# A two-layer diffusion backbone on one core: the start, the order of the input chunks, the queueing of small VectorE work, and the last chunk pairs of layer 1 in halves of 128 tokens

## What is computed

```python
for l in range(DEPTH):
    sh1, sc1, gt1, sh2, sc2, gt2 = adaln(c, w_ada[l], b_ada[l])
    hx = modulate(rms_norm(x, g_mix[l]), sh1, sc1)
    hc = modulate(rms_norm(ctx, g_mix[l]), csh1, csc1)
    px = split_cols(hx @ w_in[l], IN_SIZES)
    ...
    x = x + gt1 * mixer_output(px, y_attn, ...)
    x = x + gt2 * conv_ffn(modulate(rms_norm(x, g_ffn[l]), sh2, sc2), w_up[l], ...)
return rms_norm(x, g_final)
```

## Time and profile before

| | us |
|---|---|
| median of three runs | 1308.53 (1308.24 to 1309.39) |
| profiled execution | 1308.54 |
| its span in the trace | 1306.8 |
| PE busy | 1260.5 |
| DVE busy | 884.4 |
| ACT busy | 550.9 |
| POOL busy | 291.7 |
| granted TensorE clock, mean | 0.991 |

### The profile page before, as it was taken

The page is one execution under the profiler, slowest core; times in us unless marked ns, Lnnn a source line. Parts: engine busy times, 40 slices in busy tenths (PEclk is TensorE's granted clock), DMA queues, the critical chain, the costliest instruction groups (busy, mean ns, idle before and its releaser), DMA issues.

```text
span 1306.8 us, 20012 instructions
## 1 busy us (share of the span) xinstructions
PE 1260.5 (96%) x7718; PEld 1092.8 (84%) x7718; DVE 884.4 (68%) x1205; ACT 550.9 (42%) x872; POOL 291.7 (22%) x247
## 2 busy tenths in 40 slices
PE   4999999999999999999999999989989998999997
PEld 3788777777788798888888888989878998999997
DVE  4698678753699777662889664475676666665654
ACT  4322255553423245331223342344566645643543
POOL 0003699210233001111001110003871230220220
PEclk8999999999999999999999999999999998999999
DMA  9466311222366425662646663245333543664560
GB/s 376 155 224 201 121 61 61 73 65 76 108 201 242 124 71 183 190 216 76 205 161 195 195 216 134 66 125 174 114 105 100 194 160 130 200 217 139 183 209 33
DMA packets 50339, 198.76 MB, mean 152 GB/s; under 512 B 5584, under 2 KB 6992, under 8 KB 49104
## 3 DMA queue, kind: packets, MB, share of 16 engines
q1 hardware_dynamic: 50256, 197.62, 45.9%
HBM read 196.55 MB, written 1.05 MB: 151 GB/s over the span
## 4 chain that ended last, share of the span: by engine, by line
PE 84%; DVE 9%; ACT 4%; issue 2%; DMA 0%; SPq 0%; DVEq 0%; ACTq 0%
PE psA L522 24%; PE psA L524 24%; PE psA L523 24%; DVE w_lo L1268 2%; ACT w_hi L958 2%; PE psB L522 2%; PE psB L524 2%; PE psB L523 2%; DVE acc L1549 2%; DVE small L1562 1%; PE psA L773 1%; PE psB L801 1%; PE psB L789 1%; PE psB L704 1%; PE psB L543 1%
## 5 line engine op out<-in xcount | busy, mean ns | idle before, releaser
L522 PE MATMUL psA<-h_hi,w_hi 128*128 128x256 f32 (+1 forms) x1544 | 523.7, 339 | 10.1 <-DVE w_lo L1268 4.0
L524 PE MATMUL psA<-h_hi,w_lo 128*128 128x256 f32 (+1 forms) x1544 | 516.8, 335 | 0.0
L523 PE MATMUL psA<-h_lo,w_hi 128*128 128x256 f32 (+1 forms) x1544 | 516.7, 335 | 0.0
L1268 DVE TENSOR_TENSOR w_lo<-raw,w_hi 128x1024 fp32r<-128x1024 f32 (+2 forms) x244 | 336.3, 1378 | 124.3 <-ACT w_hi L958 124.2
L958 ACT ACTIVATE w_hi<-raw 128x1024 fp32r<-128x1024 f32 (+2 forms) x244 | 277.1, 1138 | 297.6 <-PE psA L524 226.6
L522 PEld LDWEIGHTS psA<-h_hi,w_hi 128*128 128x128 f32 x1544 | 295.2, 191 | 43.9 <-issue 7.0
L524 PEld LDWEIGHTS psA<-h_hi,w_lo 128*128 128x128 f32 x1544 | 295.3, 191 | 29.1
L523 PEld LDWEIGHTS psA<-h_lo,w_hi 128*128 128x128 f32 x1544 | 295.4, 191 | 27.9 <-issue 0.2
L511 POOL TENSOR_TENSOR hid_lo<-sig,hid_hi 128x512 f32 (+3 forms) x44 | 66.8, 1519 | 475.5 <-ACT hid_hi L1233 475.5
L1289 DVE SCALAR_TENSOR_TENSOR ada_sum<-raw,csil,ada_sum 128x1024 f32<-128x1024 f32 x112 | 155.8, 1421 | 0.0
L522 PE MATMUL psA<-hid_hi,w_hi 128*128 128x256 f32 (+1 forms) x352 | 116.3, 330 | 2.1 <-DVE sig L1742 2.0
(11 more groups left out here) (194 smaller groups left out, 1484.0 us busy)
## 6 DMA issues: line engine op xcount, KB each, us to landing
raw<-w_up SPq DMA_DIRECT2D x88, 512.0 KB, 4.2
raw<-w_ada SPq DMA_DIRECT2D x80, 512.0 KB, 3.6
raw<-w_dn SPq DMA_DIRECT2D x32, 704.0 KB, 4.5
raw<-w_in SPq DMA_DIRECT2D x36, 512.0 KB, 4.2
raw<-w_at SPq DMA_DIRECT2D x24, 512.0 KB, 3.5
raw<-w_fn SPq DMA_DIRECT2D x16, 640.0 KB, 3.9
raw<-w_sc SPq DMA_DIRECT2D x16, 640.0 KB, 3.8
raw<-w_cf SPq DMA_DIRECT2D x16, 640.0 KB, 4.0
```

What stands on the lines that cost most here:

```text
L522: pe.matmul(out, w0, hi, start=first, stop=False)
L523: pe.matmul(out, w0, lo, start=False, stop=False)
L524: return pe.matmul(out, w1, hi, start=False, stop=last)
L1268: dve.tensor_tensor(w_lo[:, s, 0:tiles * P], raw[:, r, 0:tiles * P], w_hi[:, s, 0:tiles * P].bitcast(F32), ALU.subtract).then_inc(rest_don ...
```

## The change

1. **Start.** PE issues six matmuls on zeros (`keep_warm(6)`) once the second piece of x is in, two more later. `mat` is loaded behind the first piece of x; the first four chunks of `w_in` are loaded one by one behind `w_first` 1 to 4. The first adaLN product precedes the norm's spreading, the second follows; in the loop both adaLN steps run two tiles ahead, the turn behind the third chunk's product. FIRST_LAG goes from 0, 0, 1, 2 to 0, 1, 2, 3. On DVE the shift of tile c+1 stands between tmp and h_lo of tile c. POOL makes w_lo of chunks 2 and 3.
2. **Input chunks** of both layers come in the order q, Fourier, short convolution (c, x, b), k, v, Conformer; the rotations of q follow chunks 5 to 8, that of k chunk 14; the Fourier products follow chunks 10 and 12; the transposes of v chunk 15.
3. **Layer 1's input.** The context half of norm 2 is done one tile per chunk, in chunks 0 to 7 (DVE `scaled` and `shifted_rest`, ACT `shifted_head`), and k and v are whole chunks of 512 columns.
4. **Layer 1's attention.** On DVE `peak` precedes `rest`, and `weight_sum` the second tap.
5. **Halves.** Norms 3 and 4, the pairs of chunks ahead of them, the lead of "up0" and the final norm are done for tokens 0 to 127 and then 128 to 255, by the code that layer 0 uses for its two streams (`tokens`, `token_blocks`). The output is stored in four DMAs of four tiles by 128 tokens.

The constants, SP's stores and PE's part (the numbers of lines in the text are those of before):

```diff
 FIRST_LEAD = AHEAD + 1
-FIRST_LAG = [0, 0, 1, 2]
+FIRST_LAG = [0, 1, 2, 3]
...
 
-SPLIT_IN_NORM = {0: 0, 2: 1, 4: 2}
+ROT_AT = {5: 0, 6: 1, 7: 2, 8: 3, 14: 4}
 
...
-MEAN_IN, SPREAD_IN = 5, 10
+MEAN_IN = {1: 5, 2: 5, 3: 4, 4: 6}
+SPREAD_IN = {1: 10, 2: 10, 3: 10, 4: 12}
...
+def tokens(r, s):
+
+    width = SEQ if r < 3 else SEQ // 2
+    return slice(width * s, width * (s + 1))
...
-            for kk in range(KD):
-                sp.wait_ge(fin, kk + 1)
-                sp.dma_start(io["out"][:, kk, :], y_out[:, kk, :]).then_inc(stored, 16)
-            sp.wait_ge(stored, 16 * KD)
+            for i in range(4):
+                s, g = divmod(i, 2)
+                cols = tokens(2 * DEPTH, s)
+                sp.wait_ge(fin, 4 * (i + 1))
+                sp.dma_start(io["out"][:, 4 * g:4 * g + 4, cols], y_out[:, 4 * g:4 * g + 4, cols]).then_inc(stored, 16)
+            sp.wait_ge(stored, 16 * 4)
 
...
+            def keep_warm(count):
+
+                for _ in range(count):
+                    pe.matmul(psA[3][:, 0:SEQ], glu[:, 0, 0, 0:P], glu[:, 0, 0, 0:SEQ], start=True, stop=True)
+
+            pe.wait_ge(pads, 1)
...
+            keep_warm(6)
             pe.wait_ge(mats_in, 16)
...
+            pe.wait_ge(csil_done, 1)
+            first_product(0)
             pe.wait_ge(inv, 2)
             for b in range(4):
                 mm = pe.matmul(spread_bank[b // 2][:, b * P:(b + 1) * P], M("mean"), sqb[:, b * P:(b + 1) * P],
                                start=True, stop=True)
             mm.then_inc(spread, 2)
-            pe.wait_ge(csil_done, 1)
-            first_product(0)
             turn_first(0)
+            first_product(1)
+            keep_warm(2)
+            turn_first(1)
             for at_ in range(KD + max(FIRST_LAG)):
-                if at_ + 1 < KD:
-                    first_product(at_ + 1)
                 if at_ < KD:
                     pe.wait_ge(h_rest, 2 * (at_ + 1))
                 for j in range(FIRST_LEAD):
@@ -675,8 +702,10 @@
                                      kk == 0, kk == KD - 1)
                         if kk == KD - 1:
                             mm.then_inc(chunk_done, 1)
-                    if j == 0 and at_ + 1 < KD:
-                        turn_first(at_ + 1)
+                    if j == 0 and at_ + 2 < KD:
+                        first_product(at_ + 2)
+                    if j == 2 and at_ + 2 < KD:
+                        turn_first(at_ + 2)
 
...
+                    begin(st)
+                    both_streams = idx in (12, 13)
+                    if both_streams:
+                        pe.wait_ge(h_rest, 32 * layer + 16)
+                    cols = NT if both_streams else T
...
-                splits = [slice(0, T)] if r is None else [slice(SEQ * s, SEQ * (s + 1)) for s in range(T // SEQ)]
+                splits = [slice(0, T)] if r is None else [tokens(r, s) for s in range(1 if r == 2 else 2)]
...
                     begin(one)
+                cols = tokens(r, 0)
                 for one in pair:
                     for kk in range(count):
-                        mm = product(psA[one.slot][:, 0:SEQ], one, kk, hi[:, kk, 0:SEQ], lo[:, kk, 0:SEQ],
+                        mm = product(psA[one.slot][:, cols], one, kk, hi[:, kk, cols], lo[:, kk, cols],
                                      kk == 0, kk == count - 1)
                     mm.then_inc(half_done, 1)
+                cols = tokens(r, 1)
                 for i, one in enumerate(pair):
                     for kk in range(count):
-                        if count * i + kk == MEAN_IN:
+                        if count * i + kk == MEAN_IN[r]:
                             mean_square(r, 0)
-                        if count * i + kk == SPREAD_IN:
+                        if count * i + kk == SPREAD_IN[r]:
                             spread_inverse(r, 0)
-                        mm = product(last_bank[i][:, SEQ:NT], one, kk, hi[:, kk, SEQ:NT], lo[:, kk, SEQ:NT],
+                        mm = product(last_bank[i][:, cols], one, kk, hi[:, kk, cols], lo[:, kk, cols],
                                      kk == 0, kk == count - 1)
```

DVE's part:

```diff
+                            scaled(layer, which, s, kk)
                         if kk >= 1:
-                            c = kk - 1
-                            dve.wait_ge(h_head, h0 + c + 1)
-                            dve.scalar_tensor_tensor(h_lo[:, c, cols], tmp[c % 2][:, cols],
-                                                     mod[:, layer, 24 * which + c, s:s + 1],
-                                                     h_hi[:, c, cols].bitcast(F32), ALU.add, ALU.subtract)\
-                                .then_inc(h_rest, 1)
+                            shifted_rest(layer, which, s, kk - 1)
+
+            def scaled(layer, which, s, kk):
+
+                r = 2 * layer + which
+                cols, stream = tokens(r, s), stream_of(r, s)
+                if kk >= 2:
+                    dve.wait_ge(h_rest, 16 * r + KD * s + kk - 1)
+                dve.scalar_tensor_tensor(tmp[kk % 2][:, cols], X[:, kk, cols], gsc[:, which, stream, kk:kk + 1],
+                                         spread_bank[s][:, cols], ALU.mult, ALU.mult).then_inc(ht, 1)
+
+            def shifted_rest(layer, which, s, kk):
+
+                r = 2 * layer + which
+                cols, stream = tokens(r, s), stream_of(r, s)
+                dve.wait_ge(h_head, 16 * r + KD * s + kk + 1)
+                dve.scalar_tensor_tensor(h_lo[:, kk, cols], tmp[kk % 2][:, cols], mod[:, layer, 24 * which + kk, stream:stream + 1],
+                                         h_hi[:, kk, cols].bitcast(F32), ALU.add, ALU.subtract).then_inc(h_rest, 1)
 
...
-            for c in range(KD):
+            def first_shift(c):
+
                 dve.wait_ge(first_turn, c + 1)
                 dve.tensor_scalar(mod[:, 0, c, :], psB[2][:, 0:2], V("b_ada", c), None, ALU.add)
                 dve.tensor_scalar(gsc[:, 0, :, c], psB[2][:, 2:4], first_bias[:, c:c + 1], V("g_mix", c),
                                   ALU.add, ALU.mult).then_inc(first_mod, 1)
+
+            rest(Step(-AHEAD, 0), 8)
+            first_shift(0)
+            dve.wait_ge(spread, 2)
+            for c in range(KD):
                 dve.wait_ge(first_mod, c + 1)
                 if c >= 2:
...
                     cols = slice(s * SEQ, (s + 1) * SEQ)
                     dve.wait_ge(h_head, 2 * c + s + 1)
                     dve.scalar_tensor_tensor(h_lo[:, c, cols], tmp[c % 2][:, cols], mod[:, 0, c, s:s + 1],
                                              h_hi[:, c, cols].bitcast(F32), ALU.add, ALU.subtract).then_inc(h_rest, 1)
-                if c < 2:
-                    rest(Step(c + 2 - AHEAD, 0), 8)
 
             for layer in range(DEPTH):
...
-                    if st.n and not (layer and idx in SPLIT_IN_NORM.values()):
+                    if st.n:
                         rest(st, size(st, "in"))
+                    if layer and idx < KD:
+                        if idx == 0:
+                            dve.wait_ge(spread, normed(2, 1))
+                        scaled(layer, 0, 1, idx)
...
+                    if layer and idx < KD:
+                        shifted_rest(layer, 0, 1, idx)
...
+                        k = at_place(layer, place, 0) if place is not None else None
+                        if k is not None and layer:
+                            peak(k)
                         rest(st, size(st, name))
...
                                 conv_tap(2 * place)
-                            k = at_place(layer, place, 0)
-                            if k is not None:
+                            if k is not None and layer == 0:
                                 peak(k)
                             k = at_place(layer, place, LATE[layer]["value"])
                             if k is not None:
                                 attended_rest(k)
+                            if layer and place % 2:
+                                weight_sum(place // 2)
                             if 2 * place + 1 < CONF_K:
...
-                                         ALU.mult, ALU.mult).then_inc(fin, 1)
+            def final(s):
+
+                cols = tokens(2 * DEPTH, s)
+                dve.wait_ge(spread, normed(2 * DEPTH, s))
+                for kk in range(KD):
+                    dve.scalar_tensor_tensor(y_out[:, kk, cols], X[:, kk, cols], V("g_final", kk), spread_bank[s][:, cols],
+                                             ALU.mult, ALU.mult).then_inc(fin, 1)
+
+            add_stream_square(2 * DEPTH, 1)
+            final(0)
+            stream_residual(2 * DEPTH, Step(TOTAL - 1, KD - 1), 1)
+            inverse_root(2 * DEPTH, 1)
+            final(1)
 
 
```

More of the change, by code:

```diff
@@ L440, in _ @@
             pool.memset(glu[:, :, :, :], 0.0).then_inc(pads, 1)
+            for n in range(2, FIRST_LEAD):
+                pool.wait_ge(head_done, n + 1)
+                pool.wait_ge(rest_done, n)
```

(14 more changed lines are left out.)

280 lines of the change are left out of this document (120 added, 160 removed).

## The result

The changed kernel took 1315.38 us (median of 5 runs, 1314.15 to 1315.77) against 1308.84 before (5 runs, 1308.24 to 1311.64): a ratio of 1.004, with an interval of 1.0025 to 1.0056. That is slower by 6.5 us; 1314.3 was forecast. So the sign is safe, and the size lies between 4 and 6.5.

The account below looks back on a forecast made before the run. The prediction took PE's matmul stream (busy 96%), plus the few places where PE stands still, as the bound. Its terms, 1.2 - 3.0 - 4.2 + 6.5 + 5.3 = +5.8, gave 1314.3 us, range 1298 to 1321.

Parts of the forecast that it names:

- Terms 4 and 5: Halves at layer 1's output projection with the following lead (+6.5 us), and at the program's end (+5.3 us).
- the one-column pitch: Output and final halves: 128-column matmuls start some 0.111 us apart, as one-column ones do, set by the weight load.
- the line through 256 and 512: Pitch in the halves by columns alone, from 256- and 512-column matmuls: 0.066 us at 128 columns.
- Rival (a): In the halves, loads hide and columns count: 128 columns cost 0.066 us, time 1297.2 us; chance 0.12.
- the 81 ns: Skill page's spacing for 128-column matmuls with loads; in the halves it would give -0.9 and +1.2, time 1302.8 us.
- Rival (b): In the halves, 128-column products are done in two passes: pitch 0.22 us, time about 1354 us; chance 0.08.
- Term 2: Layer 1's input chunks: -3.0 us, a gain of 6.1 less 3.1 of new waits on DVE.
- Term 3: Layer 1's attention: -4.2 us, three quarters of 5.6 us of PE waits, by moving peak ahead.
- Term 1: Start of the kernel: +1.2 us, bounds -3 and +3; first chunk products at 21.9, chunk 4 at 62.2.
- Its ring: Start: h_lo waits behind the next tile's shift, whose turn PE issues behind chunk products; 5.4 us a step, 4.42 before.
- a first phase that ends before 58: Sign of being wrong at the start: a first phase ending before 58 us would mean the ring was misread.
- Rival (c): Small waits at start, input and attention all pay (-3, -6.1, -5.6), halves' pitch 0.107: 1303.7 us; chance 0.05.

Follow-up runs that it names:

- the seven later runs: The changed kernel itself, run again with nothing altered: median 1312.46 us, ratio 1.0029.
- halves_64_columns: The changed kernel, but layer 1's products of the halves compute only the first 64 of each 128 tokens: 1345.27 us.
- hlo_first_peak_late: hlo_first with layer 1's peak back behind w_lo and the first tap, weight_sum still ahead of the second tap: 1296.28 us.
- hlo_first: The changed kernel with norms 3 and 4 whole again and, at the start, DVE's h_lo ahead of the next tile's shift: 1292.43 us.

## Why the prediction was right

The sign, the size (+5.8 forecast; +6.5 measured, +3.9 in the seven later runs) and the two large terms held. Two of the small terms were off by 3.6 and 2.7 us in opposite directions. That they nearly cancel, and the sum comes within 0.7, is luck.

**Terms 4 and 5** held to 0.1 us: 28.6 for 28.6 and 23.4 for 23.37. The choice of the one-column pitch as price of 128 columns, against the line through 256 and 512, was the step that carried the prediction; `halves_64_columns` and the products with loads of 32 columns show it right. Rival (a) is refuted. So is, for these fp32 products, the 81 ns of the Trainium skill's "TensorE: Matmul & The Clock Gate", section "Back-to-back issue gap": the trace has 0.111 through both streams, of 240 and 132 matmuls. Rival (b), two passes, is refuted by the same rows. The risk that the clock falls during the halves was in no term; it didn't occur in the runs of this kernel.

**Term 2** (-3.0) measured -3.3. What is late next was DVE, as said: L762 is PE's rotation product, which waits 1.6 for DVE's earlier rotations (forecast 1.7), and L721 the Fourier product, which waits 0.6 for the last one (forecast 1.1). The 0.7 put down to issue was there before too.

**Term 3** (-4.2) measured -6.3 in the attention: all waits went, not three quarters, and 0.6 more in the Conformer chunks behind it, where a transpose had waited 0.5. The quarter that I held back for the chain's own operations wasn't on the path. The term also laid both waits to `peak`, and one of them hangs on `weight_sum`: by `hlo_first_peak_late` `peak` is worth some 2.8, and `weight_sum`, of which the forecast had said nothing, the other 4. With the mechanism as told, the term would have been too large, not too small.

**Term 1** (+1.2, range to +3) measured +4.8, beyond its own upper bound. Its ring was right (5.18 a step for 5.4; first product 21.56 for 21.9; `hlo_first` removes it and 9.9 us go), and where the clock was low for only some 3 us, chunk 4 came at 62.80 for 62.2. Its sum failed in this trace because it priced every step at full clock, and the clock was at half for 10 us (before has 7, 24.9 to 31.9). The two long steps are 2.4 and 1.9 longer than 5.2; of the first one's 2.4, POOL's hold on h_lo, which the forecast didn't price either, is up to 1.8. The sign of being wrong that the prediction names, a first phase that ends before 58, would not have caught this: it ended late.

Rival (c), that all the small waits pay, had the attention right and nothing else.
